# A hybrid decoder layer on one core: the unread transposition in every pass of the panel loops

## The reference

```python
proj = x @ w_in[l]
q, k, v, rx, ry, gl = jnp.split(proj, SPLIT_POINTS, axis=-1)
y_attn = sliding_window_attention(q, k, v, attn_sinks[l]) @ w_attn_proj[l]
rx = causal_dwconv(rx, rnn_conv_w[l], rnn_conv_b[l])
hr = rg_lru(rx, lru_wa[l], lru_ba[l], lru_wi[l], lru_bi[l], lru_lambda[l])
y_rnn = (hr * jax.nn.gelu(ry, approximate=True)) @ w_rnn_proj[l]
g_attn, g_rnn = jnp.split(jax.nn.sigmoid(gl + b_gate[l]), 2, axis=-1)
mix = (g_attn * y_attn + g_rnn * y_rnn) @ w_out[l]
x = layer_norm(ALPHA * x + mix, ln1_g[l], ln1_b[l])
up = x @ ffn_w_up[l]
gate = causal_dwconv(x @ ffn_w_gate[l], ffn_conv_w[l], ffn_conv_b[l])
f = (jax.nn.gelu(gate, approximate=True) * up) @ ffn_w_down[l]
x = layer_norm(ALPHA * x + f, ln2_g[l], ln2_b[l])
```

## Time and profile before

| | |
|---|---|
| time, median of 3 runs | 1716.88 us (1714.54 to 1720.45) |
| profiled execution, its own time | 1706.05 us |
| its span, first to last instruction | 1704.3 us |
| mean granted TensorE clock | 0.995 |
| TensorE busy with matmuls | 1670.5 us, 98% |
| VectorE busy | 1025.1 us, 60% |
| ScalarE busy | 843.6 us, 49% |
| settle (L319) | 3 executions, 272 ns median |

### The profile page before, as it was taken

One profiled execution on the slowest core, in us unless ns is written; L12 is line 12 of the kernel. 1 busy time (PEld: TensorE's weight loads), 2 busy tenths in 40 slices (PEclk: granted clock), 3 DMA queues, 4 the chain that ended last, 5 costly groups with the idle time before them and its releaser, 6 DMA issues.

```text
span 1704.3 us, 32117 instructions
## 1 busy us (share of the span) xinstructions
PE 1670.5 (98%) x13023; PEld 1592.7 (93%) x13023; DVE 1025.1 (60%) x1190; ACT 843.6 (49%) x1027; POOL 31.3 (2%) x30
## 2 busy tenths in 40 slices
PE   7999999999999999999998999999999999999996
PEld 7999999999999999999888999998889999999885
DVE  5696695444446666656557666665444666666556
ACT  5567566444346666644436454454333444444332
POOL 0000000000000000000000000000000000000002
PEclk9999999999999999999999999999999999999998
DMA  8465463565644344455764665565665556665551
GB/s 305 146 210 169 154 210 129 194 221 192 204 149 153 127 170 134 162 188 189 290 197 149 197 197 190 189 238 197 197 197 189 189 191 196 197 197 187 190 193 72
DMA packets 157142, 317.15 MB, mean 186 GB/s; under 512 B 6008, under 2 KB 11800, under 8 KB 156312
## 3 DMA queue, kind: packets, MB, share of 16 engines
q1 hardware_dynamic: 157080, 316.28, 55.8%
HBM read 314.16 MB, written 2.10 MB: 186 GB/s over the span
## 4 chain that ended last, share of the span: by engine, by line
PE 92%; DVE 4%; ACT 3%; issue 1%; DMA 1%; SPq 0%; DVEq 0%; ACTq 0%
PE bank L268 67%; PE bank L295 20%; PE bank L489 2%; ACT s_buf L796 1%; PE bank L560 1%; PE bank L547 1%; PE bank L280 1%; DVE s_buf L1037 1%; DMA raw<-in_w_in_dram 1%; ACT w_hi L239 1%; DVE smax L1041 1%; ACT ln_t L854 0%; PE bank L538 0%; DVE res L1248 0%; DVE res L1244 0%
## 5 line engine op out<-in xcount | busy, mean ns | idle before, releaser
L246 DVE TENSOR_TENSOR w_lo<-raw,w_hi 128x1024 fp32r<-128x1024 f32 (+1 forms) x552 | 693.5, 1270 | 572.2 <-ACT w_hi L239 572.2
L268 PE MATMUL bank<-act_t,w_hi 128*128 128x256 f32 x5952 | 1025.2, 278 | 9.2 <-DVE w_lo L246 9.1
L239 ACT ACTIVATE w_hi<-raw 128x1024 fp32r<-128x1024 f32 (+1 forms) x552 | 600.1, 1096 | 711.3 <-PE bank L268 509.5
L268 PEld LDWEIGHTS bank<-act_t,w_hi 128*128 128x128 f32 x5952 | 899.1, 188 | 14.2 <-issue 6.8
L268 PE MATMUL bank<-act_t,w_lo 128*128 128x256 f32 x2976 | 823.8, 277 | 0.0
L268 PEld LDWEIGHTS bank<-act_t,w_lo 128*128 128x128 f32 x2976 | 560.1, 188 | 0.0
L295 PE MATMUL bank<-w_hi,f_t 128*128 128x512 f32 x768 | 236.7, 389 | 0.0
L295 PEld LDWEIGHTS bank<-w_hi,f_t 128*128 128x128 f32 x768 | 144.2, 188 | 29.9
L295 PE MATMUL bank<-w_lo,f_t 128*128 128x512 f32 x384 | 149.4, 389 | 0.0
L268 PE MATMUL bank<-g_t,w_hi 128*128 128x256 f32 x640 | 109.0, 276 | 0.0
L268 PEld LDWEIGHTS bank<-g_t,w_hi 128*128 128x128 f32 x640 | 96.6, 188 | 0.0
(11 more groups left out here) (139 smaller groups left out, 937.3 us busy)
## 6 DMA issues: line engine op xcount, KB each, us to landing
raw<-in_w_in_dram SPq DMA_DIRECT2D x52, 1024.0 KB, 5.1
raw<-in_ffn_w_gate_dram SPq DMA_DIRECT2D x48, 1024.0 KB, 5.1
raw<-in_ffn_w_up_dram SPq DMA_DIRECT2D x48, 1024.0 KB, 5.2
raw<-in_ffn_w_down_dram SPq DMA_DIRECT2D x48, 1024.0 KB, 5.1
raw<-in_w_in_dram SPq DMA_DIRECT2D x32, 1280.0 KB, 6.0
raw<-in_w_rnn_proj_dram SPq DMA_DIRECT2D x16, 1280.0 KB, 6.1
raw<-in_w_attn_proj_dram SPq DMA_DIRECT2D x16, 1024.0 KB, 5.0
raw<-in_w_out_dram SPq DMA_DIRECT2D x16, 1024.0 KB, 5.1
```

Of the source, the lines that this page charges most:

```text
L239: nc.scalar.activation(w_hi[:, slot, 0:size], raw[:, chunk, half:half + size], ACT.Copy)\
L246: nc.vector.tensor_tensor(w_lo[:, slot, 0:size], raw[:, chunk, half:half + size], w_hi[:, slot, 0:size].bitcast(F32), ALU.subtract).then_i ...
L268: last = nc.tensor.matmul(dst, w[:, slot, at_ % size:at_ % size + P], moving[:, kt, part, :], start=(kt == 0 and n == 0 and c % 2 == 0), s ...
```

## The change

`settle()` now stands in every pass of the loops of feature panels, except those of gr and ga, which carry attention. In the recurrence it stands at the head of passes 1 to 3, in q, rnn and attn at the head of each iteration, and in ff0 and ff1 before each up panel. The one before ff1's loop stays. In executions: 3 + 2 + 2 + 2 + 6 + 1 + 6 = 22.

```diff
-            def recurrence(i, during_x=lambda j: None):
+            def recurrence(i, during_x=lambda j: None, before=lambda: None):
 
 
                 pe.wait_ge(gates_read, i * GRP + 1)
                 pe.wait_ge(acc_free, i * 2 + 1)
+                before()
                 panel_features(pe, i * 16, 0, ACC[0], act_t, 4, 640, between=during_x)
...
             with pe.Fori(1, 4) as i:
-                recurrence(i)
+                recurrence(i, before=settle)
 
             with pe.Fori(0, 2) as i:
...
                     if pp == 0:
 
                         pe.wait_ge(gates_read, 4 * GRP + 1)
+                        settle()
                     panel_features(pe, i * 16 + UNITS["q"], 8 * pp, acc_of("q", pp), act_t, 4, 512)
...
             pe.wait_ge(g_lo, 4)
-            settle()
             with pe.Fori(0, 2) as i:
                 for pp in range(2):
                     pe.wait_ge(acc_free, i * 2 + (PANELS["rnn"] + pp + 1))
+                    if pp == 0:
+                        settle()
                     panel_features(pe, i * 16 + UNITS["rnn"], 8 * pp, acc_of("rnn", pp), g_t, 5, 512)
...
             pe.wait_ge(o_lo, NH // 2 + 1)
-            settle()
             with pe.Fori(0, 2) as i:
                 for pp in range(2):
                     pe.wait_ge(acc_free, i * 2 + (PANELS["attn"] + pp + 1))
+                    if pp == 0:
+                        settle()
...
                 with pe.Fori(0, 6) as i:
                     for pp in range(2):
                         pe.wait_ge(acc_free, i * 2 + (PANELS[f"ff{half}"] + pp + 1))
+                        if pp:
+                            settle()
```

## The result

The changed kernel takes 1733.18 us (median of 5 runs, 1731.75 to 1736.18). The kernel before took 1716.88 us beside it (5 runs, 1713.60 to 1722.65). The ratio is 1.0088, 95% interval 1.0046 to 1.0130. The prediction was 1718.1 us, with a range of 1707 to 1724. Between the two profiled executions the difference is larger, 1704.3 to 1734.4 us of span, 30.1 us. The ratios here leave out executions more than 1.5% above the fastest one of the same kernel (of the kernel before 10 of 83, all at the same granted clock as the rest), the medians don't, so the ratios of the experiments make the kernel before look a little faster than its medians do.

The account below looks back on a forecast made before the run. TensorE, busy 98% of the span, was taken as the bound. Added transpositions +2.1 us and slow stretches ended −0.9 us gave +1.2 us on the timed median 1716.88: 1718.1 us, range 1707 to 1724.

Parts of the forecast that it names:

- The size of the instruction: All 22 places: one added transposition lasts 272 ns but adds 0.13 us to TensorE's stream; the 19 add +2.1 us.
- the terms that stops were to swallow: q's first iteration: its 0.13 us free before the stop; recurrence: three together 0.2 us, partly swallowed by short stops.
- What it may give back: q's second iteration: transposition ends a 117.8 ns stretch, saving 1.7 us every other execution; −0.9 us, bounds 0 and −1.7.
- Rival 2: Feed-forward loops chiefly: the transposition itself leaves 117.8 ns a matmul; 1728.5 us with one loop, 1738 with both; chance 0.12.
- Rival 1: First feed-forward loop chiefly: timed runs hold 117.8 ns stretches, which the change removes; 1709 us, up to 1712; chance 0.38.
- Rival 3: TensorE's clock: lone transpositions count as stops, each half-clock stretch costing 1.7 us; one more likely at most, 1719.8; chance 0.04.

## Why the prediction was wrong

**The size of the instruction was right.** 0.46 us to the second group behind it against 0.47 forecast, x22, 271 ns; no added stretch at half clock. This part of the sum, +2.1 us, stands but for the terms that stops were to swallow. The stop before q's fifth unit did shrink, from 2.13 us to 1.87, but the unchanged kernel had it at 1.57 in its second profile, so this confirms nothing.

**The step that failed** is "What it may give back", the term of −0.9 us with bounds 0 and −1.7: that a transposition can end the slow gait was read off 386.37, where the stream ahead was slow, and it was taken for a property of the instruction. In the sum nothing was put down for the other direction, a stream that is fast already and turns slow. But by the prediction's own reading all stretches that got a new transposition were fast, and the trace of before has all 19 places at 113.3 ns, so the only thing that a jolt could do there was harm. In place of −0.9 us it came to some +27.9 us between the profiled executions, and to 16.3 − 2.1 = 14.2 us between the medians, which fits timed runs of before that hold slow stretches of their own.

**Rival 2 is what happened**, given 0.12. Its point of decision was right (680 slow matmuls; there are some 6200 more). Its argument against was two good outcomes: 386.37 stands behind kv's mixed stream and 1298.21 behind 512 columns. Neither stood between L268 and L268 in the fast gait, where all 19 new ones went by the profile of before. In the changed kernel's trace all seven that were entered from a fast L268 stream were followed by the slow gait; with the kernel without those in the feed-forward loops (4 of 4) and the one with 128 rows inside the panel (5 of 6) it is 16 of 17. The row that did bear on it, was given too little weight. It also spoke of one loop or both, not of a cycle, so its 1728.5 and 1738 bracket the 1733 only by luck.

**Rival 1 was half right.** Executions of the kernel before do differ by slow stretches that begin at a stop, as the second profile shows for one; for the timed runs it is inferred. But the change doesn't take them out: it replaces a scatter of 1714 to 1723 on this chip (1705 to 1741 on all) by a steady 1732 to 1736 in its five runs. The 32-row one inside every pass comes nearest to what rival 1 thought this one would do.

**Rival 3 fell**: two stretches at half clock in each trace ahead of the end, one at the start and one behind a stop, q's before and ff0's now.

What stays open is why there are two gaits at all. The runs show that the outcome depends on the kind of interruption and on what ran ahead of it (the same instruction gives other outcomes behind other streams and with 95 or 94 matmuls between). That it is the moment in a short grid at which the stream starts again fits this, but no run measures such a grid, nor which part of TensorE would make it. Also open is why a stop of the same 0.30 us ends either way in the layer; stops that short were not tried alone.

## What to carry to other kernels

Before adding anything to a stream that is the bound, read its pace from the distances between starts, and ask in which gait it runs at just that place: an instruction that cures a slow stretch can spoil a fast one, and the outcome holds for thousands of matmuls. When timed runs scatter by 2% and the profile lies at their lower end, take a second profile before drawing on the first. A disturbance is chosen by measuring it alone in a short kernel, from each entry that it will meet, and then checked in place: three in a row gave fast 12 times of 12 alone inside 256-column matmuls, and slow at both places in q.

## What the runs showed of the hardware that was not expected

- The same stream of 256-column fp32r matmuls with a weight load each runs at 113.3 or 117.8 ns. Each held for all of ff1, 2304 matmuls at clock 1.00 (fast in the kernel before, slow in the one without the three transpositions), and both appear in the lone kernel too, in pieces of 11 us, with no other engine at work and the DMAs busy 1%.
- The 512-column stream has three paces: 226.7 ns, 228.9 (out before) and 233.3 ns (out in the changed kernel), from the distances between starts. Alone it ran at 233.3 behind a slow stream 3 times of 3 and at 228.8 behind a fast one 9 of 9. In the layer the gait ahead doesn't settle it: behind a slow attn, out ran at 233.3 in three traces and at 228.9 in the one with 128 rows inside the panel, and the down projections ran at 226.7 behind either gait.
- A lone 128-row transposition between such matmuls gives slow, slow, slow, fast, in order, in a lone kernel with 96 matmuls between, and in the feed-forward loops of the changed kernel; with 95 or 94 between, or one unit further back in the panel, the order is another. A 32-row one gave fast in 10 of 10 alone behind 256-column matmuls (slow 3 of 3 behind 512) and, in the two kernels with it, 29 of 30; it costs 0.40 us, three times as much as the 128-row one.
- A hardware loop's branch doesn't disturb the stream: in the kernel before starts keep their 113 or 114 ns across the iterations of ff1, and of ff0 behind its last stop.
